# Expert down weights loaded as one 8192-byte run per partition, with the activation transposes reading every second column

## The chip, the cores and the metric

The kernel runs on one core of a Trainium2 chip. The metric is the device time of one execution in microseconds (us), the median over the runs shown.

## What is computed

A two-layer decoder trunk in float32 on 256 tokens of width 1024: each layer has gated mixers, cross-attention and a feed-forward part, dense in layer 0 and a top-2-of-8 mixture of experts in layer 1. The change touches the experts alone:

```python
def swiglu(h, wg, wu, wd):
    return (jax.nn.silu(h @ wg) * (h @ wu)) @ wd

def moe_ffn(h, w_router, wg, wu, wd):
    ...
    for e in range(N_EXPERTS):
        out = out + gate[:, e:e + 1].astype(hf.dtype) * swiglu(hf, wg[e], wu[e], wd[e])
    return out.reshape(b, s, d)
```

`wg[e]` and `wu[e]` are 1024 x 3584, `wd[e]` is 3584 x 1024, all float32: 44.04 MB an expert, 352.3 MB in all.

## The kernel before

Up to the router, weights come in units of up to 1 MB into six raw buffers, are split on ScalarE and VectorE into two float32r parts, and TensorE multiplies them in three passes.

The expert part works differently. It makes one visit per expert (and more, if an expert has more than 96 tokens; in this run there are eight visits). A visit gathers the expert's tokens into at most 96 slots (`gather`, L1612), in `n_groups` groups of 32: three groups in visits 0, 2, 3, 5 and 6, two in visits 1, 4 and 7 (`LIGHT`). Its weights are 42 units of 1 MB (`BODY`), used straight as float32. The list `order` sets the order in which units are both loaded and used: gate and up units by pairs of 512-column chunks, the down units of a chunk pair one pair later. The 21 slots (`MR`) are a ring: unit i goes into slot i mod 21.

SyncE issues every load (`load_expert_unit`, L415; L404 for the four mixed gate/up units of the last chunk). `slot_wait` (L417 to L420) lets it issue a unit only when TensorE has used the unit 21 places before. A gate, up or down unit is 256 rows of 1024 columns (4096 bytes); partition p gets rows p and 128 + p, as two runs:

```python
dst = t.rearrange("p (k n) -> p k n", k=kk)
sp.dma_start(dst, src.rearrange("e (k p) n -> p (e k) n", p=P))...
```

For a gate or up unit these rows are 14,336 bytes apart in HBM. For a down unit the 256 rows are one contiguous megabyte.

On TensorE `gate_up` (L1635) uses 32 token slots as the stationary operand and 256 weight columns as the moving one, in the four 32-column strips of the array. ScalarE takes the silu, VectorE multiplies (`act_rows`, L1255) and leaves `act_tok`: partition 32q + s holds slot s and strip q's 256 of the pair's 1024 feed-forward columns, one group of slots behind the other along the free side. `act_t_` (L1639 on, the transposes at L1650) transposes it in 128-column pieces, six in a heavy visit's call and four in a light one's, four calls a visit; `act_tok` is the stationary operand there and the identity the moving one. ScalarE copies the result to `actT` (or `actT_end` for the last chunk), and `down` (L1667) uses 32-column slices of it as the stationary operand against the down unit. The first piece of a pair belongs to the unit's row half k = 0, the second to k = 1.

TensorE runs one program in order; each unit's first matmul waits for its slot's semaphore (`unit_landed`), and its last tells SyncE that the slot is free. After the last visit there is a tail of some 15 us: scatter, final norm and store.

Of the kernel before, what the change touches and what calls it, by code (L numbers as in the profile page):

```python
# [27 lines left out]
P = 128  # L28
# [4 lines left out]
MR = 21  # L33
# [14 lines left out]
def trunk(nc, a, out):  # L48
# [9 lines left out]
    C = 512  # L58
# [64 lines left out]
    def place(name, shape, dt, where=None):  # L123
        size = 4
        for s in shape[1:]:
            size *= s
        if where is None:
            where = at["top"]
            at["top"] += (size + 63) // 64 * 64
        place_of[name] = where  # L130
        return nc.alloc_sbuf_tensor_at(name, shape, dt, offset=where)
# [17 lines left out]
    ident = place("ident", [P, P], F32)  # L149
# [41 lines left out]
    def moe(name, shape, dt, region):  # L191
        t = place(name, shape, dt, region[0])
        n = 4
        for s in shape[1:]:
            n *= s
        region[0] += (n + 63) // 64 * 64
        assert region[0] <= region[1], name
        return t
# [8 lines left out]
    act_t = moe("act_tok", [P, SG * 256], F32, work)  # L207
# [43 lines left out]
    def moe_raw(i):  # L251
        return slot_t[i % MR][:]
# [11 lines left out]
    with contextlib.ExitStack() as ctx:  # L264
# [4 lines left out]
        moe_loaded = [ctx.enter_context(nc.semaphore(f"moe_loaded{i}")) for i in range(MR)]  # L269
# [8 lines left out]
        def tiles_of(c, n=4):  # L278
            return pair(c)[:, 0:n * SEQ].rearrange("p (d t) -> p d t", t=SEQ)
# [46 lines left out]
        def every(v, per, n):  # L326

            return v * per + n
# [22 lines left out]
        with nc.Block() as block:  # L351
# [3 lines left out]
            def _(sp):  # L355
# [39 lines left out]
                def load_expert_unit(i, e):  # L395
                    t = moe_raw(i)
                    w, g, part = order[i]
                    j, n = GROUPS[g]
                    if w == "both":
                        k = 2 * part  # L400
                        dst = t.rearrange("p (k h n) -> p k h n", k=2, h=2)
                        for h, name in enumerate(("w_e_gate", "w_e_up")):
                            src = a[name][0][bass.ds(e, 1), k * P:(k + 2) * P, j * C:(j + 1) * C]
                            sp.dma_start(dst[:, :, h, :], src.rearrange("e (k p) n -> p (e k) n", p=P)  # L404
                                         ).then_inc(moe_loaded[i % MR], 16)
                        return
                    if w == "down":
                        k, kk = 4 * j + 2 * part, 2
                        src = a["w_e_down"][0][bass.ds(e, 1), k * P:(k + kk) * P, :]
                    else:  # L410
                        kk = 2
                        k = kk * part
                        src = a["w_e_" + w][0][bass.ds(e, 1), k * P:(k + kk) * P, j * C:(j + n) * C]
                    dst = t.rearrange("p (k n) -> p k n", k=kk)
                    sp.dma_start(dst, src.rearrange("e (k p) n -> p (e k) n", p=P)).then_inc(moe_loaded[i % MR], 16)  # L415

# [5 lines left out]
                def load(e, v):  # L422
                    for i in range(BODY):
                        slot_wait(i, v)
                        load_expert_unit(i, e)


                for i in range(MR):
                    if i == 1:

                        sp.wait_ge(s["unit_used"], mix_start[-1])
                    elif i == 4:

                        sp.wait_ge(s["o_done"], NH * DEPTH)
                    elif 7 <= i < 7 + RAW:
                        sp.wait_ge(s["lo_ready"], U0 - RAW + i - 7 + 1)
                    elif 7 + RAW <= i < 7 + RAW + 2 * SPL:
                        sp.wait_ge(s["unit_used"], U0 - SPL + (i - 7 - RAW) // 2 + 1)
                    elif i == MR - 1:

                        sp.wait_ge(s["hg_ready"], NT)
                    load_expert_unit(i, FIRST)
                for i in range(MR, BODY):
                    slot_wait(i, 0)
                    load_expert_unit(i, FIRST)
# [860 lines left out]
            def _(pe):  # L1306
                p = At()
# [124 lines left out]
                for l in range(DEPTH):  # L1432
# [7 lines left out]
                    for g in range(NG):  # L1440
                        ins = pe.matmul(tiles_of(p.c)[:, g, :], wpg[:, g, :], pp[:, g, :], start=True, stop=True)
# [34 lines left out]
                    for h in range(NH):  # L1476
# [6 lines left out]
                        for t in range(NT):  # L1483
                            for d in range(2):
                                ins = pe.matmul(b[:, t * SEQ:(t + 1) * SEQ], qT[:, 2 * h + d, t * P:(t + 1) * P],
                                                kT[:, 2 * h + d, :], start=d == 0, stop=d == 1)
# [88 lines left out]
                def logits(k):  # L1575

                    ready(k)
                    for n, h in enumerate((Mh, Ml)):
                        for t in range(NT):
                            ins = pe.matmul(bank(3)[:, 2 * t * NE:2 * (t + 1) * NE], h[:, k, t * P:(t + 1) * P], wr2[:, k, :],  # L1580
                                            start=k == 0 and n == 0 and t == 0, stop=k == KD - 1 and n == 1,
                                            skip_group_check=True)
                    return ins
# [7 lines left out]
                for k in range(KD // 2, KD):  # L1591
                    ins = logits(k)
# [47 lines left out]
                def act_t_(g, v, n_groups):  # L1640

                    pe.wait_ge(s["act_ready"], every(v, NG4, g + 1))
                    if g == 0:
                        pe.wait_ge(s["xadd_done"], every(v, 4, 4))
                        pe.wait_ge(s["st_ready"], every(v, 1, 1))
                    else:
                        pe.wait_ge(s["actT_ready"], every(v, NG4, g))
                    o = ps[:, 6:8, :].rearrange("p a b -> p (a b)")
                    for f in range(2 * n_groups):
                        ins = pe.transpose(o[:, f * P:(f + 1) * P], act_t[:, f * P:(f + 1) * P], ident[:])  # L1650
                    ins.then_inc(s["t_done"], 1)

                def down(i, v, n_groups):
# [33 lines left out]
                def visit(v, n_groups=SG, more=True):  # L1687
                    for i in range(BODY):
                        (down if order[i][0] == "down" else gate_up)(i, v, n_groups)
                        for n in range(4):  # L1690
                            if i == SCATTER_AFTER[n]:
                                if n < 2:
                                    pe.wait_ge(s["y_ready"], every(v, 2, n + 1))
                                else:

                                    pe.wait_ge(s["xadd_done"], every(v, 4, n - 1))
                                scatter(n, v)
                        if i == ST_AFTER:
                            pe.wait_ge(s["xadd_done"], every(v, 4, 4))

                            pe.wait_ge(s["gatev_ready"], 1)
                            for t in range(NT):
                                pe.transpose(bank(7)[:, t * P:(t + 1) * P], S[:, t, :], ident[:])
                            for t in range(NT):
                                ins = pe.matmul(bank(7)[:, SEQ:SEQ + 1], S[:, t, :],
                                                gatev[:, t, bass.ds(every(v, 1, 0), 1)], start=t == 0, stop=t == NT - 1)
                            ins.then_inc(s["ts_done"], 1)
                        for g in range(NG4):
                            if i == T_AFTER[g]:
                                act_t_(g, v, n_groups)  # L1710
                        if more and i == DOWN[-1] - 1:
                            gather(every(v, 1, 2))
# [107 lines left out]
```

## Time and profile before

| what | value |
|---|---|
| median of 3 runs | 1588.34 us (1587.67 to 1588.65) |
| the profiled execution's own time | 1587.19 us |
| its span, first to last instruction | 1585.5 us |
| TensorE busy | 1564.2 us (99% of the span) |
| expert units, first use to last | 723 to 1570 us |
| mean DMA rate from 844 to 1490 us | 399 to 406 GB/s |

The profiled execution is 1.15 us under the median. Its time has 1.7 us outside the span. In the profile, PE is TensorE's matmuls, PEld its loads of the stationary operand (which overlap matmuls), SPq the time SyncE's sequencer spends on issuing. In a label `ps<-ident,act_tok` the moving operand stands first and the stationary one second.

### The profile page before, as it was taken

The numbers are of one execution on the slowest core, as the hardware profiler recorded it, in microseconds if no ns is written. First come the engines' busy times: TensorE is split into PE (matmuls) and PEld (weight loads), VectorE is DVE, ScalarE is ACT, GpSimd is POOL, SyncE is SP. The second block draws the span as 40 slices with busy tenths as digits, with TensorE's granted clock in tenths as the row PEclk, the third lists the DMA queues.
The fourth block names the chain that finished last, engine by engine and source line by source line (L and its number), as shares of the span: only waits on it lengthen the run. The fifth ranks groups of instructions, "written<-read, shape, count | busy, mean of one in ns | idle before, by whom it ended". The sixth has DMA issues, their size and how long they took to land. (4 is left out here: it accounts for less than half of the span.)

```text
span 1585.5 us, 42325 instructions
## 1 busy us (share of the span) xinstructions
PE 1564.2 (99%) x19683; PEld 1186.0 (75%) x19683; DVE 498.8 (31%) x563; ACT 412.3 (26%) x502; POOL 33.4 (2%) x119
## 2 busy tenths in 40 slices
PE   8999999999999999999999999999999999999996
PEld 7999898998989998986666566666665656656654
DVE  4555656455456646544002020010020100110202
ACT  5444455443345443541001010010010100100102
POOL 1000000000000000103000000000000000000000
PEclk9999999999999999999999999999999999999998
DMA  9555643556565555579999999999999999999995
GB/s 349 177 175 185 219 160 107 167 176 222 160 206 185 177 173 189 194 281 400 374 389 373 402 408 405 405 408 396 408 407 390 408 407 387 407 406 396 408 394 216
DMA packets 164693, 479.41 MB, mean 302 GB/s; under 512 B 9028, under 2 KB 14244, under 8 KB 164516
## 3 DMA queue, kind: packets, MB, share of 16 engines
q1 hardware_dynamic: 164516, 476.69, 80.2%
q8 instruction: 155, 2.54, 0.7%
q14 instruction: 22, 0.18, 0.0%
HBM read 475.61 MB, written 1.05 MB: 301 GB/s over the span
## 5 line engine op out<-in xcount | busy, mean ns | idle before, releaser
L1635 PE MATMUL ps<-slot,h_slots 128*32 128x256 f32 x9408 | 523.7, 380 | 0.0
L1635 PEld LDWEIGHTS ps<-slot,h_slots 128*32 128x32 f32 x9408 | 299.8, 110 | 205.2 <-issue 13.0
L924 DVE TENSOR_TENSOR wlo<-raw,whi 128x2048 fp32r<-128x2048 f32 (+1 forms) x116 | 259.0, 2236 | 210.5 <-ACT whi L595 210.5
L1332 PE MATMUL ps<-a_hi,whi 128*128 128x256 f32 x992 | 281.4, 284 | 0.0
L1332 PE MATMUL ps<-a_hi,wlo 128*128 128x256 f32 x992 | 280.7, 283 | 0.0
L1332 PE MATMUL ps<-a_lo,whi 128*128 128x256 f32 x992 | 280.7, 283 | 0.0
L595 ACT ACTIVATE whi<-raw 128x2048 fp32r<-128x2048 f32 (+1 forms) x116 | 216.9, 1870 | 164.5 <-PE ps L1332 107.6
L1667 PE MATMUL ps<-slot,actT 128*32 128x256 f32 x4032 | 223.6, 379 | 0.0
L1667 PEld LDWEIGHTS ps<-slot,actT 128*32 128x32 f32 x4032 | 130.2, 110 | 86.5 <-issue 1.3
L1332 PEld LDWEIGHTS ps<-a_lo,whi 128*128 128x128 f32 x992 | 190.4, 192 | 0.1
L1332 PEld LDWEIGHTS ps<-a_hi,whi 128*128 128x128 f32 x992 | 190.4, 192 | 0.1
L1332 PEld LDWEIGHTS ps<-a_hi,wlo 128*128 128x128 f32 x992 | 190.4, 192 | 0.0
L1255 DVE TENSOR_TENSOR act_tok<-silu_tmp,ps 128x768 f32<-128x768 f32 (+3 forms) x32 | 27.4, 855 | 493.5 <-PE ps L1635 341.9
L595 ACT ACTIVATE actT<-ps 128x768 f32<-128x768 f32 (+1 forms) x24 | 17.5, 731 | 565.4 <-PE ps L1650 565.4
L1241 DVE TENSOR_TENSOR x_res<-x_res,ps 128x512 f32<-128x512 f32 x32 | 21.3, 685 | 96.8 <-PE ps L1677 96.8
L1352 PE MATMUL ps<-whi,a_hi 128*128 128x512 f32 x128 | 50.6, 396 | 1.1 <-DVE a_lo L929 1.1
L1352 PE MATMUL ps<-whi,a_lo 128*128 128x512 f32 x128 | 49.9, 390 | 0.0
L1352 PE MATMUL ps<-wlo,a_hi 128*128 128x512 f32 x128 | 49.9, 390 | 0.0
L871 ACT ACTIVATE silu_tmp<-ps 128x768 f32<-128x768 f32 (+3 forms) x32 | 23.2, 726 | 74.9 <-PE ps L1635 74.9
L1332 PE MATMUL ps<-mem_hi,whi 128*128 128x256 f32 x128 | 37.5, 293 | 2.4 <-DVE wlo L924 2.4
L1667 PE MATMUL ps<-slot,actT_end 128*32 128x256 f32 x672 | 38.1, 380 | 0.4 <-DMA slot<-in_w_e_down 0.4
L1332 PE MATMUL ps<-mem_lo,whi 128*128 128x256 f32 x128 | 37.1, 290 | 0.0
(245 smaller groups left out, 1360.4 us busy)
## 6 DMA issues: line engine op xcount, KB each, us to landing
slot<-in_w_e_down SPq DMA_DIRECT2D x112, 1024.0 KB, 17.9
slot<-in_w_e_gate SPq DMA_DIRECT2D x96, 1024.0 KB, 18.4
slot<-in_w_e_up SPq DMA_DIRECT2D x96, 1024.0 KB, 18.5
raw<-in_w_in SPq DMA_DIRECT2D x32, 1024.0 KB, 5.4
slot<-in_w_e_gate SPq DMA_DIRECT2D x32, 512.0 KB, 8.6
slot<-in_w_e_up SPq DMA_DIRECT2D x32, 512.0 KB, 12.4
raw<-in_w_xk SPq DMA_DIRECT2D x8, 1024.0 KB, 5.2
raw<-in_w_xv SPq DMA_DIRECT2D x8, 1024.0 KB, 5.0
```

The source lines that it names most:

```text
L595: return act.activation(dst, src, ACT.Copy, scale=scale)
L871: act.activation(silu_t[to, 0:w], ps[of, 0:2, :].rearrange("p a b -> p (a b)")[:, 0:w], ACT.Silu).then_inc(s["silu_ready"], 1)
L924: dve.tensor_tensor(wlo[n % SPL][:, 0:size], raw[n % RAW][:, 0:size], whi[n % SPL][:, 0:size].bitcast(F32), ALU.subtract).then_inc(s["lo_r ...
L1241: dve.tensor_tensor(xs, xs, bank(6 + n % 2), ALU.add).then_inc(s["xadd_done"], 1)
L1255: dve.tensor_tensor(act_t[of, 0:w], silu_t[of, 0:w], ps[of, b0:b0 + 2, :].rearrange("p a b -> p (a b)")[:, 0:w], ALU.mult).then_inc(s["act ...
L1332: ins = pe.matmul(o[:, d, :], w[wi][:, k, d * P:(d + 1) * P], xs[xi][:, k0 + k, :], start=first and d % 2 == 0, stop=last, skip_group_chec ...
L1352: ins = pe.matmul(o[:, t, 0:nn], xs[xi][:, k0 + k, t * P:(t + 1) * P], w[wi][:, k, :], start=j == 0 and k == 0 and n == 0, stop=j == n_uni ...
L1635: ins = pe.matmul(o[q * QP:(q + 1) * QP, h * n:(h + 1) * n], he[:, kt, h * QP:(h + 1) * QP], w[:, k, q * n:(q + 1) * n], start=kt == 0 and ...
L1667: ins = pe.matmul(o[q * QP:(q + 1) * QP, h * 256:(h + 1) * 256], lhs, w[:, k, q * 256:(q + 1) * 256], start=g == 0 and f == 0 and h % 2 == ...
```

## The change

A down unit is now loaded so that partition p holds rows 2p and 2p + 1, next to each other both in HBM and in the slot: one run of 8192 bytes. The transposes read every second column of `act_tok` (even columns for k = 0, odd ones for k = 1), so that row p of the transposed piece belongs to row 2p + k of the unit. Gate, up and mixed units, the matmuls, the waits and the order of the instructions on every engine stay as they are.

```diff
@@ load_expert_unit
                     if w == "down":
-                        k, kk = 4 * j + 2 * part, 2
-                        src = a["w_e_down"][0][bass.ds(e, 1), k * P:(k + kk) * P, :]
-                    else:
-                        kk = 2
-                        k = kk * part
-                        src = a["w_e_" + w][0][bass.ds(e, 1), k * P:(k + kk) * P, j * C:(j + n) * C]
+
+                        k = 4 * j + 2 * part
+                        src = a["w_e_down"][0][bass.ds(e, 1), k * P:(k + 2) * P, :].rearrange("e (p k) n -> p (e k n)", p=P)
+                        sp.dma_start(t, src).then_inc(moe_loaded[i % MR], 16)
+                        return
+                    kk = 2
+                    k = kk * part
+                    src = a["w_e_" + w][0][bass.ds(e, 1), k * P:(k + kk) * P, j * C:(j + n) * C]
@@ act_t_
                     o = ps[:, 6:8, :].rearrange("p a b -> p (a b)")
+                    rows_of = act_t[:].rearrange("p (h n k) -> p h k n", k=2, n=P)
                     for f in range(2 * n_groups):
-                        ins = pe.transpose(o[:, f * P:(f + 1) * P], act_t[:, f * P:(f + 1) * P], ident[:])
+                        ins = pe.transpose(o[:, f * P:(f + 1) * P], rows_of[:, f // 2, f % 2, :], ident[:])
```

## Rows read from the trace of the kernel before

**Rows 1.** The page: TensorE's busy time, its granted clock and the DMA by fortieths.
```profile
PE 1564.2 (99%) x19683; PEld 1186.0 (75%) x19683; DVE 498.8 (31%) x563; ACT 412.3 (26%) x502; POOL 33.4 (2%) x119
...
PEclk9999999999999999999999999999999999999998
DMA  9555643556565555579999999999999999999995
```

**Rows 2.** Windows cut at the visits' borders: one heavy, two light, the tail.
```profile
core 0: us, PE busy (x) PEld busy (x) DVE busy (x) ACT busy (x) POOL busy (x), PEclk, DMA share, GB/s
...
844.00:927.00 83.00, 83.00 (x1410) 50.00 (x1406) 10.78 (x21) 8.58 (x18) 0.00 (x0) 1.00 1.03 405
...
1370.00:1490.00 120.00, 120.00 (x2090) 72.66 (x2086) 11.87 (x21) 10.33 (x17) 0.00 (x0) 1.00 1.03 403
1490.00:1570.00 80.00, 79.55 (x1382) 46.48 (x1370) 9.86 (x18) 8.13 (x16) 0.00 (x0) 1.00 0.95 372
1570.00:1585.50 15.50, 3.62 (x11) 2.12 (x8) 8.26 (x12) 6.87 (x15) 3.35 (x6) 0.74 0.17 68
```

**Rows 3.** TensorE's waits over the span: us in total, times, longest.
```profile
PE ps L1414 <- POOL const_rows L479: 3.6, 1, 3.6
...
PE ps L1667 <- DMA slot<-in_w_e_down: 0.4, 1, 0.4
```

**Rows 4.** Timeline of PE in visit 5: start us, us, line, operation, count.
```profile
1285.45 10.57 PE L1635 MATMUL ps<-slot,h_slots 128*32 128x256 f32 x192
1295.84 10.54 PE L1667 MATMUL ps<-slot,actT 128*32 128x256 f32 x192
...
1327.86 10.54 PE L1667 MATMUL ps<-slot,actT 128*32 128x256 f32 x192
```

**Rows 5.** Timeline of SyncE's issues, visit 5's second set of downs and visit 7's last.
```profile
1293.59 10.48 SPq L415 DMA_DIRECT2D slot<-in_w_e_down  x4
...
1541.43 9.58 SPq L415 DMA_DIRECT2D slot<-in_w_e_down  x6
```

**Rows 6.** DMA issues of the page: count, KB each, median us to landing.
```profile
slot<-in_w_e_down SPq DMA_DIRECT2D x112, 1024.0 KB, 17.9
slot<-in_w_e_gate SPq DMA_DIRECT2D x96, 1024.0 KB, 18.4
```

**Rows 7.** Timeline of PE at the end of visit 7.
```profile
1563.40 0.66 PE L1650 MATMUL ps<-ident,act_tok 128*128 128x128 f32 x4
1563.99 1.93 PE L1667 MATMUL ps<-slot,actT 128*32 128x256 f32 x32
1565.74 1.91 PE L1667 MATMUL ps<-slot,actT_end 128*32 128x256 f32 x32
1568.10 1.93 PE L1667 MATMUL ps<-slot,actT_end 128*32 128x256 f32 x32 [0.45 <-DMA slot<-in_w_e_down]
```

**Rows 8.** DMA queue from 1060 to 1085 us (packets, MB, share of 16 engines): full queue.
```profile
q1 hardware_dynamic: 2636, 10.16, 101.8%
```

**Rows 9.** DMA queue from 100 to 140 us, where rows of 2048 bytes are loaded.
```profile
q1 hardware_dynamic: 3692, 7.34, 54.2%
```

**Rows 10.** Source L1650, the transposes: duration ns min/median/max, first and last start.
```profile
L1650 PEld LDWEIGHTS ps<-ident,act_tok x168: 138/140/144, 758.1 to 1563.7; 128*128 128x128 f32 x168
L1650 PE MATMUL ps<-ident,act_tok x168: 272/273/331, 758.1 to 1563.8; 128*128 128x128 f32 x168
```

**Rows 11.** Timeline around one call of six transposes in visit 2.
```profile
1020.14 0.64 PEld L1650 LDWEIGHTS ps<-ident,act_tok 128*128 128x128 f32 x6 [0.41 <-issue]
1020.14 0.87 PE L1650 MATMUL ps<-ident,act_tok 128*128 128x128 f32 x6
...
1020.95 0.42 PE L1635 MATMUL ps<-slot,h_slots 128*32 128x256 f32 x4
```

**Rows 12.** Groups of PEld: the load of a 128-column float32 operand outside transposes.
```profile
L1612 PEld LDWEIGHTS ps<-sel_tok,h_tok 128*128 128x128 f32 x256 | 29.2, 192 | 2.9 <-issue 2.9
```

## The prediction

> **What bounds the kernel now.** I read the page first, for the engine that is full, then the windows cut at the visits, then what TensorE waited for, and last the timelines of SyncE and TensorE side by side, to see how far loads run ahead of use. TensorE is busy 99% of the span at a granted clock of full speed, 2.4 GHz, in all slices but the last, and the DMA is full too from two fifths of the span on [rows 1]. Two full engines ask which of them waits for the other. Inside the visits TensorE has no idle time before 1490 us [rows 2], and in the whole span it waits for a load once, for 0.4 us, in `down` [rows 3]. So TensorE sets the pace of the experts. Its pace is steady: 192 matmuls, four heavy units, from 1285.45 to 1295.84 us are 54.1 ns each, 2.60 us a unit [rows 4]; in the light last visit 32 matmuls from 1563.99 to 1565.74 us are 54.7 ns each, 1.75 us a unit [rows 7].
>
> The DMA is hardly behind. At 403 GB/s [rows 2] a visit's 44.04 MB take 109 us. TensorE needs 120 us for a heavy visit and 83 us or less for a light one, so loads gain some 11 us on it in a heavy visit and lose 26 us or more in a light one. How much lead is left is read from pairs: the downs issued from 1293.59 us on [rows 5] land 17.9 us later by the median [rows 6], the first at about 1312 us, and TensorE starts on these same four at 1327.86 us [rows 4]: 16 us of lead. The last six downs are issued between 1541.43 and 1551.01 us [rows 5], and TensorE takes the very last at 1568.10 us after 0.45 us of waiting [rows 7]: the lead is used up just as the work ends. What follows, 15.5 us of tail [rows 2], is untouched. So the end is held by TensorE, and by the DMA almost to the same microsecond: **slower loads would show at once, faster loads hardly at all.**
>
> **The change part by part.** Nothing changes its order on any engine, and no wait is added. Two things change their form.
>
> *The down loads.* 112 units [rows 6] become 128 runs of 8192 bytes each in place of 256 of 4096. What one engine takes for a run: on the full queue 101.8% of 16 engines for 25 us is 407.2 us, for 10.16 MB / 4096 = 2480 runs, 164 ns each, short packets neglected [rows 8]; where rows of 2048 bytes are loaded, 54.2% of 16 engines for 40 us is 346.9 us for 3584 runs, 97 ns each [rows 9]. So doubling the bytes adds 67 ns and a run has some 30 ns that don't grow. A run of 8192 bytes then takes 30 + 4 x 67 = 298 ns (an estimate from these rows) against 328 for two of 4096. A down unit has eight such runs per engine: 8 x 30 = 240 ns saved, 9% of it. Bounds: no gain at all (8192 bytes travel as two of 4096), 328 ns; and nothing in these rows excludes a loss, for no load before has a run over 4096 bytes. I take 298, since both measured sizes lie on that side.
>
> What it is worth: the loads run against a full queue from visit 2 on, that is for 6 x 14 = 84 of the downs, so the DMA would finish 84 x 0.24 = 20 us earlier. TensorE can take only what it waits for, 0.45 us [rows 7]. The rest becomes lead that nobody uses, and DMA engines that stand idle while SyncE waits for a free slot. Term: **-0.45 us**. The runs' median is 1.15 us over the profiled execution; if that is all waiting for loads at the end, which no row shows, the gain would be up to 1.6 us.
>
> Here a rule of the Trainium skill can be weighed. The trace moves 399 to 408 GB/s over long stretches. The page "DMA: Bandwidth & Descriptors", section "Bandwidth", says that HBM binds a core's loads at about 358 GB/s, with 435 GB/s as the ceiling of the way into SBUF. By the first figure longer runs could gain nothing and the DMA term would be 0; the trace already stands above it, so that rule does not hold here. The second leaves room for the 298 ns (16 x 8192 bytes in 298 ns is 440 GB/s, just about the ceiling).
>
> *The transposes.* There are 168 (24 in a heavy visit, 16 in a light one), each with a load of the stationary operand of 140 ns and a matmul of 273 ns [rows 10]. They overlap: from 1020.14 to 1020.95 us for six [rows 11] and 0.59 us for four [rows 7] makes 110 ns for each further one. They stand in TensorE's own stream, so whatever the strided read costs is added in full, 168 times. That the strided operand is the stationary one is read from the label. No row shows a strided operand on TensorE. Bounds: nothing; as much as brings the load from 140 to the 192 ns of the slowest sort of 128-column float32 load in this trace [rows 12], 168 x 52 ns = 8.7 us; and, far out, a load that takes twice its 140 ns, 168 x 140 = 23.5 us. A gain is excluded: no read gets shorter. I take nothing, because a load of 128 columns of float32 is slow already (140 to 192 ns), and the nearest row for the same instruction is its own.
>
> On this the skill has a rule that could speak against the change. The page "SBUF — State Buffer", section "Door 1", says that SBUF is read in lines of 16 bytes and that full rate needs at least two hits in a line. Every second float32 is 8 bytes apart from the next, just two hits, so the rule allows it and its sum is the same 0; with one hit a line it would speak for rival A. No row before the change shows it.
>
> *SyncE.* An issue of a down takes a few us only because the queue is full (10.48 us for four [rows 5], the pace of the DMA); with faster loads it gets shorter. Nobody waits for it but TensorE through the slots. Term 0, covered by the lead of some 10 us or more in every visit but the last.
>
> Sum: 1587.19 - 0.45 = 1586.74 us against the profiled execution; on the median of the runs, 1588.34 - 0.45 = **1587.9 us**. A measurement of this kernel can tell about 0.2%, 3.2 us, from no change.
>
> **The rivals.**
>
> *A, the strided load of the stationary operand costs time (slower).* Place: the transposes (L1653 of the changed kernel), 168 times, in TensorE's stream. For it: TensorE has no slack in the visits [rows 2], and a stationary load is part of the 110 ns. Against it: the identity's matmul also fills those 110 ns, so a load that grows a little may stay hidden. It decides from 3.2 us / 168 = 19 ns each. At 52 ns each: 1588.3 + 8.7 - 0.45 = 1596.6 us. If the whole 110 ns doubled: 168 x 110 = 18.5 us, 1606 us. Chance 0.15.
>
> *B, a run of 8192 bytes is slower than two of 4096 (slower).* An engine that holds one run longer, or another spread of the addresses over HBM: now neighbouring partitions are 8 KB apart. Since the lead is used up at the end, each ns per run ends up in the time: 84 units x 8 runs = 672 in a row, 0.67 us per ns. It decides from 328 + 5 ns. At 5% longer (344 ns): + 11 us, 1599 us. Against it: the two sizes measured. Chance 0.04.
>
> *C, nothing happens to the packets.* The 8192 bytes travel as two packets of 4096. The DMA's times stay as they are, 1588.3 us. Within the same bound as the forecast; chance 0.12.
>
> *D, TensorE itself is held up by the loads, and gets faster with them.* Then the 54.1 ns of a matmul would hide waits. Against it: heavy and light visits, with 16 us of lead and with none, show 54.1 and 54.7 ns. It would need 3.2 us, 0.4% of 847 us. Chance 0.03, for about 1583 us.
>
> **How the numbers follow.** The forecast (loads faster, transposes free, 1587.9) has 0.66, C 0.12, A 0.15, B 0.04, D 0.03. Forecast and C lie within 0.2%: same 0.78. A and B: slower 0.19. Faster 0.03. The range begins at the largest gain the forecast allows, 1588.3 - 1.6 less the spread of the runs, 1586.2, and reaches up to A with 52 ns, 1596.9, so that the bound of the unknown cost lies inside. The likeliest case alone would be 1586.5 to 1589.
>
> **What would show it.** Packets of q1 fall by 112 x 128 = 14,336 (C: they don't), and the DMA's rate in the downs rises over 408 GB/s. The landing time of the downs stays or falls; the 0.45 us of waiting at 1568 us is gone, and the last visits' DMA share falls under full. L1653's loads stay at 140 ns and six transposes at 0.81 us: if they are longer, A is true by exactly 168 times the difference. Heavy visits last 120 us as before. The prediction would be wrong if a call of transposes grew by over 0.1 us, or if TensorE waited for `slot<-in_w_e_down` more than now.

## The result and the profile after

| | before | after |
|---|---|---|
| median of 19 runs each | 1587.6 us | 1590.43 us |
| ratio, 95% interval | | 1.0015 (1.0009 to 1.0021) |
| the profiled execution's own time | 1587.19 us | 1591.05 us |
| its span | 1585.5 us | 1589.3 us |
| its last expert matmul ends | 1570.03 us | 1573.71 us |

The changed kernel is slower by 2.8 us, 0.15% (0.09 to 0.21%). The page's lines on the engines and on the DMA queue; the first stands against [rows 1], and the queue's line before read `q1 hardware_dynamic: 164516, 476.69, 80.2%`:

```profile
PE 1568.6 (99%) x19683; PEld 1192.5 (75%) x19683; DVE 498.8 (31%) x563; ACT 412.1 (26%) x502; POOL 33.3 (2%) x119
...
q1 hardware_dynamic: 150180, 476.69, 79.5%
```

The packets of q1 fell from 164,516 to 150,180, by 14,336 = 112 x 128: the down units do travel as runs of 8192 bytes. PEld is 6.5 us busier with the same number of loads. Where it went is seen at the transposes, against [rows 10] (duration in ns, min/median/max):

```profile
L1653 PEld LDWEIGHTS ps<-ident,act_tok x168: 194/209/219, 759.1 to 1568.0; 128*128 128x128 f32 x168
L1653 PE MATMUL ps<-ident,act_tok x168: 281/283/388, 759.1 to 1568.1; 128*128 128x128 f32 x168
```

The strided load of the stationary operand takes 209 ns in place of 140. In the timeline (start us, duration us), six transposes now need from 1022.17 to 1023.09 us, 0.92 us against 0.81 in [rows 11]:

```profile
1022.17 0.80 PEld L1653 LDWEIGHTS ps<-ident,act_tok 128*128 128x128 f32 x6 [0.41 <-issue]
1022.17 0.98 PE L1653 MATMUL ps<-ident,act_tok 128*128 128x128 f32 x6
1023.09 0.16 PEld L1637 LDWEIGHTS ps<-slot,h_slots 128*32 128x32 f32 x8
1023.09 0.42 PE L1637 MATMUL ps<-slot,h_slots 128*32 128x256 f32 x4
```

That is 18 ns for each of six, and 20 for each of four at the end of the last visit (1567.64 to 1568.31 us below against 0.59 us in [rows 7]); times 168, 3.0 to 3.4 us. It shows in every visit: from its first expert matmul to the next visit's, a heavy one takes 120.6 us in place of 120.2, a light one 83.4 in place of 83.0. The end of visit 7, against [rows 7]:

```profile
1567.64 0.74 PE L1653 MATMUL ps<-ident,act_tok 128*128 128x128 f32 x4
1568.31 1.93 PE L1670 MATMUL ps<-slot,actT 128*32 128x256 f32 x32
1570.07 3.64 PE L1670 MATMUL ps<-slot,actT_end 128*32 128x256 f32 x64
```

The wait for the last down is gone. The experts start here, first before, then after:

```profile
723.13 3.23 PE L1635 MATMUL ps<-slot,h_slots 128*32 128x256 f32 x56
```

```profile
724.16 2.15 PE L1637 MATMUL ps<-slot,h_slots 128*32 128x256 f32 x36
```

From the first expert matmul to the end of the last one it was 1570.03 - 723.13 = 846.90 us, and is 1573.71 - 724.16 = 849.55 us: + 2.65 us. The profiled executions differ by 3.8 us of span, though. The tail after the experts has 0.1 us of the rest, and the start 1.03 us, which arises in the first 25 us, long before the changed lines run: ScalarE's split that starts at 24.65 us before starts at 25.72 us after. Windows of the start, before first, then after; PEclk is the third column from the end:

```profile
14.00:21.00 7.00, 4.57 (x22) 4.42 (x21) 6.06 (x6) 7.00 (x15) 0.85 (x3) 0.52 1.09 364
21.00:24.00 3.00, 3.00 (x27) 3.00 (x26) 2.55 (x3) 0.70 (x1) 0.41 (x1) 0.99 1.03 378
```

```profile
14.00:21.00 7.00, 4.58 (x22) 4.34 (x23) 6.06 (x6) 7.00 (x15) 0.53 (x2) 0.65 1.09 363
21.00:24.00 3.00, 3.00 (x19) 3.00 (x19) 2.14 (x3) 1.11 (x1) 0.74 (x2) 0.67 1.04 380
```

Before, TensorE was granted 0.52 of its clock from 14 to 21 us, nearly all of it at the lower level, 1.2 GHz, and 2.4 GHz from there. After, the low stretch falls later and reaches into the window in which TensorE is full: 19 matmuls fit in the 3 us in place of 27. In the profiles of this study the experts start between 0.3 us earlier and 1.3 us later than before, whichever the edits, and the tail behind them lasts 14.9 to 15.7 us. The whole span of a single profiled pair is therefore no measure of 1 us here. The expert part is one: a heavy visit's 120.2 us agree within 0.02 us between the kernel before and the three kernels below whose matmuls and transposes are as before.

### The profile page after: what moved, and what is told of

Its sections match the earlier page's. It is cut to its first block and busy times, and to the rows that moved or that the text cites. A ratio compares the mean times of both kernels' runs of the same rounds, so it can differ in the third digit from the quotient of the medians.

```text
span 1589.3 us, 42325 instructions
## 1 busy us (share of the span) xinstructions
PE 1568.6 (99%) x19683; PEld 1192.5 (75%) x19683; DVE 498.8 (31%) x563; ACT 412.1 (26%) x502; POOL 33.3 (2%) x119
## 3 DMA queue, kind: packets, MB, share of 16 engines
q1 hardware_dynamic: 150180, 476.69, 79.5%
```

## The experiments

Theory S: the strided load of the stationary operand is the whole cost, and the longer runs only remove the last wait. Theory L: the longer runs disturb TensorE or come in worse. All ratios are to the kernel before on the same chip, with their 95% intervals.

### The new loads alone

Against the changed kernel:

```diff
-                    rows_of = act_t[:].rearrange("p (h n k) -> p h k n", k=2, n=P)
...
-                        ins = pe.transpose(o[:, f * P:(f + 1) * P], rows_of[:, f // 2, f % 2, :], ident[:])
+                        ins = pe.transpose(o[:, f * P:(f + 1) * P], act_t[:, f * P:(f + 1) * P], ident[:])
```

> The new loads alone: down units as 128 runs of 8192 bytes, the transposes reading neighbouring columns as before (so the downs multiply rows of the weights that do not belong to the transposed columns; all durations stay meaningful). Theory S (the strided load of the stationary operand is the whole cost): 0.0 to 1.0 us under the kernel before, median near 1587.1; loads of the transposes 140 ns, six of them 0.81 us; no wait for slot<-in_w_e_down at the end; some 9 us of lead there. Theory L (the longer runs disturb TensorE or arrive worse): 2 to 3 us over the kernel before, with the transposes' loads near 209 ns although nothing is strided, or other PE groups longer.

Measured: 1586.37 us against 1588.11, ratio 0.9993 (0.9984 to 1.0002). The transposes' loads are back at 140 ns, and TensorE waits for no load. The end of visit 7 in its timeline:

```profile
1563.19 0.66 PE L1652 MATMUL ps<-ident,act_tok 128*128 128x128 f32 x4
1563.78 1.94 PE L1669 MATMUL ps<-slot,actT 128*32 128x256 f32 x32
1565.53 3.64 PE L1669 MATMUL ps<-slot,actT_end 128*32 128x256 f32 x64
```

From the first expert matmul (722.91 us) to the last one's end (1569.16 us) it is 846.25 us, 0.65 less than before. That is the last wait: in [rows 7] the second 32 matmuls on `actT_end` start 2.36 us after the first, where 32 take 1.75, so 0.61 us go with the wait that the profile puts at 0.45. The visits before the last keep their length (120.2 and 83.0 us). Theory L falls: the new loads alone cost nothing, and gain 0.65 us in the profile. The interval of the runs reaches across 1. The last down lands some 6 us ahead of its use.

### The stride alone

```diff
+                    rows_of = act_t[:].rearrange("p (h n k) -> p h k n", k=2, n=P)
...
-                        ins = pe.transpose(o[:, f * P:(f + 1) * P], act_t[:, f * P:(f + 1) * P], ident[:])
+                        ins = pe.transpose(o[:, f * P:(f + 1) * P], rows_of[:, f // 2, f % 2, :], ident[:])
```

> The stride alone: the transposes read every second column, the loads are those of before (again columns and weight rows that do not belong together). Theory S: 168 transposes cost 18 to 20 ns more each, 3.0 to 3.4 us; the wait of 0.45 us at the end disappears under them, since the loads get that much more time, so + 2.6 to + 3.3 us, 1590.4 us. Loads of the stationary operand at about 209 ns. Theory L: no difference, 1587.6 us, with loads at 140 ns.

Measured: 1590.4 us against 1588.11, ratio 1.0015 (1.0006 to 1.0024): the whole change's ratio, with the old loads.

```profile
L1651 PEld LDWEIGHTS ps<-ident,act_tok x168: 194/209/219, 758.0 to 1566.9; 128*128 128x128 f32 x168
```

The expert part takes 849.54 us (723.06 to 1572.60), as in the changed kernel, and TensorE waits for no load although these are the old ones: with 3 us more work on TensorE the loads are in time, 2.5 us ahead at the end. The stride's own price is read between the two kernels that wait for no load, the changed one and the new loads alone: 849.55 - 846.25 = 3.30 us, 19.6 ns for each of 168 transposes. So the gain of the new loads does not add up with the cost of the stride. Once the stride is there, longer runs save nothing at all.

### The stride moved to VectorE

Against the changed kernel:

```diff
-                    dve.tensor_tensor(act_t[of, 0:w], silu_t[of, 0:w],
-                                      ps[of, b0:b0 + 2, :].rearrange("p a b -> p (a b)")[:, 0:w],
+                    cols_of = lambda t: t.rearrange("p (h n k) -> p h n k", n=P, k=2)
+                    dve.tensor_tensor(act_t[of, 0:w].rearrange("p (h k n) -> p h n k", n=P, k=2), cols_of(silu_t[of, 0:w]),
+                                      cols_of(ps[of, b0:b0 + 2, :].rearrange("p a b -> p (a b)")[:, 0:w]),
                                       ALU.mult).then_inc(s["act_ready"], 1)
```

(The transposes are those of before, the loads those of the change.)

> The whole job with the stride moved from TensorE to VectorE: loads as in the change, act_rows reads silu_tmp and PSUM in the order of the columns but writes even columns and odd columns to separate halves of each 256, and the transposes read neighbouring columns. Theory S: transposes back at 140 ns per load and 0.81 us for six, TensorE waits nowhere, 0.0 to 1.0 us under the kernel before (1587.1 us). VectorE's multiply may grow from 0.95 to as much as 1.9 us; it has over 3 us before the transposes in the tightest place (the last group), so it costs nothing. Theory L: 1590 us as the change.

Measured: 1586.1 us against 1588.11, ratio 0.9989 (0.998 to 0.9998), 2.0 us under the kernel before and the lowest median of all. Of these 2.0 us the mechanism explains 0.65: the expert part takes 846.25 us, the same as with the new loads alone, whose median is 1586.37 us. The rest is not explained by the edit; the start and the tail of an execution move by as much between kernels that are alike there. The multiply, min/median/max in ns, was 686/954/958 before:

```profile
L1258 DVE TENSOR_TENSOR act_tok<-silu_tmp,ps x32: 1103/1587/1605, 747.3 to 1559.3; 128x768 f32<-128x768 f32 x15, 128x512 f32<-128x512 f32 x9, 64x768 f32<-64x768 f32 x5, 64x512 f32<-64x512 f32 x3
```

The widest form (768 columns) grew by 0.63 us, the mean of the 32 from 855 to 1411 ns, on an engine that is idle most of a visit. That delays nothing: visits take 120.2 and 83.0 us as before.

### Down units in runs of 2048 bytes

```diff
+                        dst = t.rearrange("p (k h n) -> p k h n", k=2, h=2)
+                        for h in range(2):
+                            src = a["w_e_down"][0][bass.ds(e, 1), k * P:(k + kk) * P, h * C:(h + 1) * C]
+                            sp.dma_start(dst[:, :, h, :], src.rearrange("e (k p) n -> p (e k) n", p=P)
+                                         ).then_inc(moe_loaded[i % MR], 16)
+                        return
...
-        LOADS = [32 if w == "both" else 16 for w, _, _ in order]
+        LOADS = [32 if w in ("both", "down") else 16 for w, _, _ in order]
```

> The kernel before with every down unit loaded by two transfers of 512 columns each, so in runs of 2048 bytes: a test of the step that slower loads show at once because the lead is used up at the end. By packets of 2048 bytes at 85 to 97 ns against 4096 at 164, a down unit takes 0.1 to 0.5 us longer, 84 of them 9 to 40 us: 1597 to 1628 us, with waits for slot<-in_w_e_down in the light visits, the last above all. If TensorE alone sets the time and the DMA has slack that the packets' times don't show: under 1590 us.

Measured: 1600.14 us, ratio 1.0077 (1.0061 to 1.0092), + 12 us. TensorE's waits over the span:

```profile
PE ps L1672 <- DMA slot<-in_w_e_down: 7.0, 10, 0.9
...
PE ps L1640 <- DMA slot<-in_w_e_up: 3.6, 5, 1.5
```

The visits before the last keep their length (120.2 and 83.0 us); the last grows from 80.0 to 92.7 us. So the prediction's picture of the lead holds: slower loads show as soon as the lead is used up.

This kernel and the changed one also size the fixed part of the time that one run of bytes takes. Share of 16 engines times span is the time all packets took:

```profile
q1 hardware_dynamic: 194980, 476.70, 81.0%
```

For 2048-byte downs 0.810 x 16 x 1597.4 = 20,702 us, for 4096-byte ones 0.802 x 16 x 1585.5 = 20,345 us, for 8192-byte ones 0.795 x 16 x 1589.3 = 20,216 us. Cutting 28,672 runs of 4096 in two cost 357 us, 12 ns each; joining 14,336 pairs saved 129 us, 9 ns each (12 ns with the first experiment's 79.6% of 1584.2 us; one digit of the share is some 2 ns for a pair).

### Every third and every fourth column

Why does a stride of two cost anything, and what does a wider one cost?

```diff
+                        at3 = P * (f // 3) + f % 3
+                        ins = pe.transpose(o[:, f * P:(f + 1) * P], act_t[:, at3:at3 + 382:3], ident[:])
```

> Loads as before; the transposes read every third column (12 bytes apart) of windows of 382 columns, so their content is no longer a transpose of the activations. Measured so far: stride 1 gives loads of 140 ns and 110 ns for each further transpose, stride 2 gives 209 and 129. Theory P (unit stride reads two float32 in one access, any other stride one, so stride 2, 3 and 4 cost the same): loads 209 ns, + 3.1 us in TensorE's stream, median 1590.4 us. Theory B (the cost goes with the bytes passed over, by 69 ns of load per further float32): loads about 278 ns, six transposes well over 1.3 us, 168 x 88 ns = 15 us more, 1602 us.

```diff
+                        at4 = 256 * (f // 4) + f % 4
+                        ins = pe.transpose(o[:, f * P:(f + 1) * P], act_t[:, at4:at4 + 509:4], ident[:])
```

> The same with every fourth column, 16 bytes apart, one element per line of 16 bytes (windows of 509 columns, content no longer a transpose). Theory P: again 209 ns and 1590.4 us. Theory B: about 347 ns, 168 x 157 = 26 us more, 1613 us. Theory H (lines of 16 bytes with at least two hits read at full rate, as the Trainium skill's page SBUF - State Buffer has it): 2 and 3 should be alike or nearly, and 4 should be much worse than both.

Measured: 1589.88 us, ratio 1.0011 (1.0002 to 1.0021), and 1589.97 us, ratio 1.0014 (1.0004 to 1.0023), against 1587.77. Source lines of the two, third column first:

```profile
L1651 PEld LDWEIGHTS ps<-ident,act_tok x168: 187/201/217, 759.3 to 1567.5; 128*128 128x128 f32 x168
```

```profile
L1651 PEld LDWEIGHTS ps<-ident,act_tok x168: 196/211/220, 758.0 to 1567.1; 128*128 128x128 f32 x168
```

209, 201 and 211 ns for strides of 2, 3 and 4: the price is that of leaving unit stride, and does not grow. In the stream it is the same: a stretch of one heavy visit with its 24 transposes, from one `gather` to the next, takes 120.17 us before and 120.61, 120.55 and 120.65 us with the three strides, 16 to 20 ns a transpose. Theory B falls, and so does H: the Trainium skill's page "SBUF — State Buffer", section "Door 1", gives full rate to two hits in a 16-byte line, and the trace disagrees twice: two hits a line (stride 2) are not free, and one (stride 4) is no worse. That unit stride reads two elements at once (theory P) fits these numbers, but nothing here shows the inside; only its forecast that the strides tried cost nearly alike is shown.

### The stride on the moving side

```diff
+    wide = place("ident_wide", [P, 2 * P], F32, place_of["strict_upper"])
...
-                fill_columns(gatev, 0.0, gate[:]).then_inc(s["gatev_ready"], 1)
+                link(fill_columns(gatev, 0.0, gate[:]))
+                pool.wait_ge(s["rank_done"], 1)
+                pool.wait_ge(s["count_done"], 1)
+                link(pool.memset(wide[:], 0.0))
+                pool.tensor_copy(wide[:, 0:255:2], ident[:]).then_inc(s["gatev_ready"], 1)
...
-                        ins = pe.transpose(o[:, f * P:(f + 1) * P], act_t[:, f * P:(f + 1) * P], ident[:])
+                        ins = pe.transpose(o[:, f * P:(f + 1) * P], act_t[:, f * P:(f + 1) * P], wide[:, 0:255:2])
```

> Loads as before, the stationary operand read with neighbouring columns as before, but the moving operand (the identity, laid out over every second column of a tile of 256 in the place of two tables that are dead by then) is read with stride 2; the result is the same. Theory M1 (only the stationary load dislikes the stride): loads 140 ns, 0.81 us for six, 1587.6 us. Theory M2 (the moving side pays as well): matmuls longer by up to 53 ns, 168 x 53 = 9 us, 1596 us. GpSimd makes the table 2 us later than gatev_ready was, with 14 us of slack.

Measured: 1588.06 us against 1587.77, ratio 1.0003 (0.9993 to 1.0013).

```profile
L1655 PEld LDWEIGHTS ps<-ident_wide,act_tok x168: 137/139/144, 758.6 to 1565.2; 128*128 128x128 f32 x168
L1655 PE MATMUL ps<-ident_wide,act_tok x168: 273/277/336, 758.6 to 1565.3; 128*128 128x128 f32 x168
```

```profile
1021.00 0.91 PE L1655 MATMUL ps<-ident_wide,act_tok 128*128 128x128 f32 x6
1021.84 2.37 PE L1640 MATMUL ps<-slot,h_slots 128*32 128x256 f32 x40
```

The load stays at 139 ns; six transposes take 0.84 us, 5 ns more each than before and not 18. M1 holds nearly: a strided moving operand costs between a quarter and a third of what the stationary one costs here, under 1 us in all, less than the runs can tell.

### The stride in plain float32 matmuls

```diff
-                            ins = pe.matmul(o, hg[:, t, k * P:(k + 1) * P], S[:, t, :], start=t == 0, stop=t == NT - 1)
+                            at2 = 2 * P * (k // 2) + k % 2
+                            ins = pe.matmul(o, hg[:, t, at2:at2 + 255:2], S[:, t, :], start=t == 0, stop=t == NT - 1)
```

> Loads and transposes as before, but the 256 matmuls of the gather (plain float32, not transposes) read their stationary 128 columns of h_tok with stride 2, so the features come out in another order and the experts' results are not the reference's. Before: loads of 192 ns, 32 matmuls in 3.76 us, 117 ns each. Theory P: 69 ns longer loads (261), of which as with the transposes some 19 to 69 ns reach the stream: 256 x 19 = 5 us to 256 x 69 = 18 us, 1592 to 1605 us. Theory T (only transposes pay): 1587.6 us.

Measured: 1589.01 us against 1587.77, ratio 1.0005 (0.9996 to 1.0015).

```profile
L1613 PEld LDWEIGHTS ps<-sel_tok,h_tok x256: 193/196/197, 720.5 to 1487.3; 128*128 128x128 f32 x128
```

```profile
1244.60 4.04 PE L1613 MATMUL ps<-sel_tok,h_tok 128*128 128x128 f32 x32
1248.57 0.64 PE L1668 MATMUL ps<-slot,actT_end 128*32 128x256 f32 x8
```

The load took 192 ns with neighbouring columns [rows 12] and takes 196 with the stride; 32 matmuls take 3.97 us in place of 3.77, 6 ns each. Neither end of the forecast: theory P's + 69 ns is missing, and T's nothing is not quite true. One reading is that this load had no short form to lose; no run tests it further.

## Why the prediction was wrong

The forecast was a gain too small to measure, - 0.45 us, with a chance of 0.78 for no measurable change; measured is + 2.8 us. That still lies under the 0.2% (3.2 us) below which the prediction speaks of no change, and in its range, but only because two opposite terms stayed small and rival A's price had been let into the range: the direction was wrong, and the term that set it. So this is no success of the mechanism. Point by point:

- *TensorE sets the pace, the DMA is level with it only at the end.* Right. Half the runs' length gave + 12 us at once, twice their length 0.65 us in the profile.
- *The down loads: -0.45 us.* Right in kind: TensorE can take no more than it waits for. The stretch of the experts became 0.65 us shorter with the new loads alone, 0.61 us of it at the last wait, of which the forecast counted 0.45. The size of the lead was wrong: 298 ns for a run of 8192 bytes rested on 97 ns for one of 2048 [rows 9], read where the DMA was half idle, and so on a window in which shares are no measure of a full queue. From the pages' totals a run has 9 to 12 ns of fixed time, not 30; the last down lands at 1561.3 us with the new loads alone, 6.7 us earlier and not 20 (672 runs in a row at 9 to 12 ns give 6 to 8 us). The time did not depend on it.
- *The transposes: 0, "because a load of 128 columns of float32 is slow already".* **This is the step that failed.** The forecast put the strided read at nothing on the strength of that sentence, and the strided read costs 3.30 us. The load of a transpose was not slow already: it was the fast sort, 140 ns, beside 192 ns for the plain one, and became 209. The bound from the nearest other row, 140 to 192 ns, was nearly what the load did (209), and rival A had the mechanism, its place and the rule that it is paid 168 times. What rival A over-priced is how much of a longer load reaches the stream: of 69 ns only 18 to 20 do; the rest adds nothing to the stream, presumably because it runs beside the neighbouring matmul. So the prediction was also wrong that the cost of the read is "added in full, 168 times": that would be 11.6 us. The "against it" there (a load that grows a little may stay hidden) was half right. At 19.6 ns each the cost lies on the very point of 19 ns from which rival A was said to decide, and a call of six grew by 0.11 us, over the 0.1 us that was to show the prediction wrong.
- *Rival B, longer runs slower:* did not happen. *Rival C, no change of packets:* did not happen. *Rival D:* did not happen; with the new loads alone a heavy visit takes 120.2 us as before.
- *The sum.* 3.30 us for the stride less 0.65 of wait is + 2.65 us, the whole of the profiled expert part, against 2.8 (1.4 to 3.3) by the runs. The two parts alone would not have been added: the stride alone also costs just this, since it too takes the wait away.
- *The rule weighed for the transposes* supported the forecast, and the runs contradict it. It should have been held against the fact that no row showed any stride on TensorE, and that this engine has no slack to hide an error in.

## What to carry to other kernels

When a layout is changed to make a transfer's runs longer, look at who pays for the other half of the change: here the stride fell on the one engine that is busy throughout, while the transfers that gained were hidden all but for the last. Put the stride where there is idle time: the same permutation in VectorE's multiply cost up to 0.63 us each, off the path, and kept the 0.65 us that the new loads gain in the profile (ratio of the runs 0.9989, 0.998 to 0.9998). And a term set to nothing because no row shows it deserves the value of the nearest row rather than a rule's word when the engine is full. The nearest row's 52 ns would have priced it at 8.7 us, 2.6 times too high but with the right sign: 168 times 19.6 ns were enough to turn it.

## What the hardware showed that was not expected

- A load of a 128-column float32 stationary operand takes 140 ns for a transpose with neighbouring columns, and 209, 201 and 211 ns with strides of 2, 3 and 4. A plain float32 matmul's takes 192 ns with neighbouring columns and 196 with stride 2. So a stride takes the transpose's advantage of 52 ns away, and 9 to 19 ns beyond it. In the stream each of six transposes costs 18 ns more, each plain matmul 6 ns, and a strided moving operand 5 ns.
- VectorE's float32 multiply of 128 x 768 went from 954 to 1587 ns when its output was written with neighbouring elements 512 bytes apart, its inputs read in order as before.
- Packets of 8192 bytes save 9 to 12 ns on two of 4096, and two of 2048 cost 12 ns more than one of 4096, as totals over the span.
- The start of an execution moves by up to 1.6 us between profiles of kernels that are the same there; where the experts start 1.0 to 1.3 us late, the stretch at 1.2 GHz reaches past 21 us (granted clock 0.63 to 0.67 from 21 to 24 us, against 0.99 before). A start 0.6 us late goes with 0.77, one 0.3 us late with 0.88. That the clock is the whole cause is not shown.
